# Step sizes moved into the exponents of a state-space scan, and one product per head in place of two

## What is computed

```python
xbc = jax.nn.silu(centred_dwconv(c_xbc, lp['ssm_conv_w']) + lp['ssm_conv_b'])
c_x, c_b, c_c = split_cols(xbc, (D_INNER, SSM_GROUPS * SSM_STATE, SSM_GROUPS * SSM_STATE))
dt = jax.nn.softplus(c_dt.reshape(b, t, 2, SSM_HEADS) + lp['ssm_dt_bias'])
da = dt * (-jnp.exp(lp['ssm_a_log']))
y_f, ss_f = ssd_scan(c_x * dt[:, :, 0, :, None], da[:, :, 0], c_b, c_c, s_ssm0[:, 0])
y_b, ss_b = ssd_scan(rev(c_x * dt[:, :, 1, :, None]), rev(da[:, :, 1]), rev(c_b), rev(c_c), s_ssm0[:, 1])
y = y_f + rev(y_b) + lp['ssm_d'][:, None] * c_x
```

```python
lmat = jnp.exp(jnp.where(lower, acum[..., :, None] - acum[..., None, :], -jnp.inf))
cb = jnp.einsum('bclgn,bcsgn->bcgls', cc, bc)
y_diag = jnp.einsum('bcgls,bcgrls,bcsgrp->bclgrp', cb, lmat, xc)
```

## Time and profile before

| what | value |
| --- | --- |
| median of 3 runs | 3850.91 us |
| range of the runs | 3846.19 to 3855.83 us |
| the profiled execution | 3846.83 us |
| its span, first to last instruction | 3845.1 us |
| mean granted TensorE clock | 0.978 of full speed |
| TensorE busy | 3655.9 us (95%), 29057 matmuls |
| TensorE weight loads | 3441.8 us (90%) |
| VectorE, ScalarE, GpSimd busy | 2042.3, 1087.7, 638.9 us |
| DMA | 506.51 MB, mean 132 GB/s |

### The profile page before, as it was taken

How to read it: one execution, slowest core, us unless ns; L and a number is a source line. 1 busy time by engine, 2 the same in 40 slices (tenths; PEclk the granted TensorE clock), 3 DMA queues, 4 the chain that set the end, 5 groups by cost and what they waited for, 6 DMA issues and landing times.

```text
span 3845.1 us, 68478 instructions
## 1 busy us (share of the span) xinstructions
PE 3655.9 (95%) x29057; PEld 3441.8 (90%) x29057; DVE 2042.3 (53%) x2526; ACT 1087.7 (28%) x1953; POOL 638.9 (17%) x698
## 2 busy tenths in 40 slices
PE   7999999999899899899989999999998998899998
PEld 6999999999888776899989999999997886588998
DVE  5531453233478786585375225523325877856743
ACT  4211111122344562331122102112224456343311
POOL 1111111222400233100011101112233003510000
PEclk8999999999899999999999999999998999999999
DMA  6332233233621387752333332333346114776432
GB/s 242 110 106 92 87 93 95 85 122 109 248 59 39 131 287 247 242 170 76 104 122 102 93 104 76 93 92 108 105 135 210 51 41 166 260 252 189 138 94 91
DMA packets 361201, 506.51 MB, mean 132 GB/s; under 512 B 82528, under 2 KB 284872, under 8 KB 357968
## 3 DMA queue, kind: packets, MB, share of 16 engines
q1 hardware_dynamic: 309880, 375.22, 29.9%
q0 software_dynamic: 35040, 103.09, 8.8%
q10 hardware_dynamic: 16000, 24.12, 1.9%
HBM read 330.62 MB, written 171.73 MB: 131 GB/s over the span
## 4 chain that ended last, share of the span: by engine, by line
PE 70%; DVE 10%; issue 9%; DMA 3%; DVEq 2%; SPq 2%; ACT 2%; POOL 2%; ACTq 0%; POOLq 0%
PE PSUM L833 10%; PE PSUM L835 10%; PE PSUM L834 10%; PE PSUM L1379 4%; PE PSUM L1381 4%; PE PSUM L1380 4%; PE PSUM L1658 4%; PE PSUM L1493 3%; PE PSUM L1480 2%; PE PSUM L1790 2%; PE PSUM L1792 2%; PE PSUM L1791 2%; PE PSUM L1459 1%; SPq L695 1%; PE PSUM L1460 1%
## 5 line engine op out<-in xcount | busy, mean ns | idle before, releaser
L833 PE MATMUL PSUM<-h_hi,w_hi 128*128 128x384 f32 x2304 | 772.1, 335 | 4.4 <-ACT conv_in L1974 1.8
L835 PE MATMUL PSUM<-h_hi,w_lo 128*128 128x384 f32 x2304 | 770.4, 334 | 0.0
L834 PE MATMUL PSUM<-h_lo,w_hi 128*128 128x384 f32 x2304 | 770.4, 334 | 0.0
L833 PEld LDWEIGHTS PSUM<-h_hi,w_hi 128*128 128x128 f32 x2304 | 432.7, 188 | 9.2 <-issue 9.1
L834 PEld LDWEIGHTS PSUM<-h_lo,w_hi 128*128 128x128 f32 x2304 | 432.7, 188 | 0.0
L835 PEld LDWEIGHTS PSUM<-h_hi,w_lo 128*128 128x128 f32 x2304 | 432.7, 188 | 0.0
L2356 POOL DMA_DIRECT2D proj_d<-leave x140 | 131.8, 942 | 1381.3 <-DVE leave L2704 543.1
L1379 PE MATMUL PSUM<-h_hi,w_hi 128*128 128x384 f32 x960 | 325.4, 339 | 0.0
L1380 PE MATMUL PSUM<-h_lo,w_hi 128*128 128x384 f32 x960 | 321.5, 335 | 0.0
L1381 PE MATMUL PSUM<-h_hi,w_lo 128*128 128x384 f32 x960 | 321.5, 335 | 0.0
L2810 DVE TENSOR_REDUCE row_max<-PSUM 128x1 f32<-128x1152 f32 x128 | 173.4, 1355 | 97.6 <-PE PSUM L1460 97.4
(11 more groups left out here) (406 smaller groups left out, 7329.5 us busy)
## 6 DMA issues: line engine op xcount, KB each, us to landing
proj_d<-leave POOLq DMA_DIRECT2D x140, 512.0 KB, 3.9
w_raw<-in_w_in SPq DMA_DIRECT2D x54, 1024.0 KB, 5.5
gdn_tile_d<-g_out SPq DMA_DIRECT2D x18, 1536.0 KB, 6.9
wide_br<-proj_d SPq DMA_DIRECT2D x48, 576.0 KB, 4.4
xs<-ssm_tok_d SPq DMA_DIRECT2D x32, 640.0 KB, 5.7
ssm_tok_d<-x_rest SPq DMA_DIRECT2D x36, 512.0 KB, 3.5
w_in<-in_w_in SPq DMA_DIRECT2D x16, 1024.0 KB, 6.3
av_t<-gdn_tile_d SPq DMA_DIRECT2D x28, 512.0 KB, 5.3
```

The costliest lines, as they stand in the source:

```text
L833: pe.matmul(dst, wh, x_hi[:, k, lo:hi], start=(k == 0), stop=False)
L834: pe.matmul(dst, wh, x_lo[:, k, lo:hi], start=False, stop=False)
L835: last = pe.matmul(dst, wl, x_hi[:, k, lo:hi], start=False, stop=(k == kt - 1))
```

## The change

The step size enters as a logarithm: exp(decay[l] - decay[s] + log dt[s]). Log dt is formed in the projection's decay pieces (Ln, and one correction step with Exp), split in two parts like the decay sums, transposed, and stored as `steprow_d`; a third DMA per direction brings it to rows 64 to 95 of `s_col`, where `s_row` (through `head_of`) has the matching sign. With dt in the exponential, x needs no scaling: VectorE adds the exponentials of both directions and multiplies the sum by `cb`, and y takes one product per head with `xt` as it is. `x_dt` goes, `w_ssm` is one tile, and the exponents go by half of the heads (both directions of a half), where they went by direction. D times x comes after all four exponentials, and x_rest on VectorE after the second half.

The decay pieces of the projection: ScalarE's D_SUMS and D_LAST, TensorE's D_LAST, VectorE's D_TERMS and D_SUMS.

```diff
+                    if run == D_SUMS:
+                        act.wait_ge(decay_term, l * 3 + 2)
+                        act.activation(dec["u"][:, :, 16:48], dec["neg"][:, :, 16:48], ACT.Ln)
+                        act.drain()
+                        act.activation(dec["poly"][:, :, 16:48], dec["u"][:, :, 16:48], ACT.Exp, scale=-1.0).then_inc(decay_exp, 1)
...
+                        act.activation(step_rows[:, 0:3], bank(6, 3 * P, P).rearrange("p (c n) -> p c n", n=P), ACT.Copy)
+                        act.activation(step_rows[:, 3], bank(7, P), ACT.Copy)
+                        act.activation(step_rows[0:64, 4], bank(7, P, P)[0:64], ACT.Copy).then_inc(row_made, 1)
...
+                        for c in range(3):
+                            pe.transpose(bank(6, P, (c + 1) * P), step_cols[:, c * P:c * P + P], ident)
+                        pe.transpose(bank(7, P), step_cols[:, 3 * P:4 * P], ident)
+                        pe.transpose(bank(7, P, P)[0:64], step_cols[:, 4 * P:4 * P + 64], ident).then_inc(decay_prod, 1)
...
+                        dve.tensor_scalar(D["neg"][:, :, 16:48], D["soft"][:, :, 16:48], 1e-37, None, ALU.max)
...
+                        dve.wait_ge(decay_exp, l * 3 + 2)
+                        steps = D["poly"][:, :, 16:48]
+                        dve.tensor_tensor(steps, D["neg"][:, :, 16:48], steps, ALU.mult)
+                        dve.drain()
+                        dve.scalar_tensor_tensor(steps, steps, -1.0, D["u"][:, :, 16:48], ALU.add, ALU.add)
+                        dve.drain()
+                        for d in range(2):
+                            dve.tensor_copy(step_hl[:, :, d, 0], steps[:, :, 16 * d:16 * d + 16])
+                        dve.drain()
+                        for d in range(2):
+                            dve.tensor_tensor(step_hl[:, :, d, 1], steps[:, :, 16 * d:16 * d + 16], step_hl[:, :, d, 0].bitcast(F32), ALU.subtract)
```

SyncE stores the new rows; every engine that waits for the rows waits for seven stores in place of five:

```diff
+                sp.dma_start(flat_steps[0:512].rearrange("(c p) n -> p c n", p=P), step_rows[:, 0:4].bitcast(F32)).then_inc(row_out, 16)
+                sp.dma_start(flat_steps[512:576], step_rows[0:64, 4].bitcast(F32)).then_inc(row_out, 16)
-                sp.wait_ge(row_out, l * 80 + 80)
+                sp.wait_ge(row_out, l * 112 + 112)
```

TensorE in SSM preparation:

```diff
                     for h in range(8 * half, 8 * half + 8):
-                        for d in range(2):
-                            for part in HALVES:
-                                dst = PSUM[part, h * SP_:(h + 1) * SP_]
-                                last = pe.matmul(dst, w_ssm[d][:, h, part], x_dt[p][d][:, h], start=d == 0, stop=d == 1)
+                        for part in HALVES:
+                            last = pe.matmul(PSUM[part, h * SP_:(h + 1) * SP_], w_ssm[:, h, part], xt[p][:, h * SP_:(h + 1) * SP_], start=True, stop=True)
...
-                def exponents(t, d):
+                def exponents(t, half):
                     n = l * NT + t
-                    if d == 0:
+                    if half == 0:
                         for e in range(2):
-                            pe.wait_ge(s_in[e], (n + 1) * 32)
-                    for half in range(2):
-                        if t or d:
-                            pe.wait_ge(sp_e, n * 4 + 2 * d + half - 1)
+                            pe.wait_ge(s_in[e], (n + 1) * 48)
+                    for d in range(2):
+                        if t or half:
+                            pe.wait_ge(sp_e, n * 4 + 2 * half + d - 1)
```

ScalarE, per tile:

```diff
-                    act.wait_ge(sp_cb, n * 2 + 1)
...
-                        for h in ((0, 1, 2, 3, 4, 5), range(6, SH))[d]:
+                        for h in ((), range(SH))[half]:
```

GpSimd, the loads of the next tile's rows and their wait:

```diff
+                    pool.dma_start(s_col[d][64:96], steprow_d[t, d]).then_inc(s_in[d], 16)
...
-                        pool.wait_ge(sp_d, (l * NT + t) * 4 - 2 + 2 * d)
+                        pool.wait_ge(sp_d, (l * NT + t) * 4 - 1 + d)
```

VectorE, per tile:

```diff
-                    times_dt(t, 0).then_inc(sp_cb, 1)
...
-                    times_dt(t, 1)
...
                         for d in range(2):
-                            dve.wait_ge(sp_e, n * 4 + 2 * d + half + 1)
-                            dve.tensor_tensor(w_ssm[d][:, hs], e_ssm[d][:, hs], again(cb[p][:, half], 8), ALU.mult).then_inc(sp_w, 1)
-                        if half == (0 if t else 1):
+                            dve.wait_ge(sp_e, n * 4 + 2 * half + d + 1)
+                        dve.tensor_tensor(e_ssm[0][:, hs], e_ssm[0][:, hs], e_ssm[1][:, hs], ALU.add)
+                        dve.drain()
+                        dve.tensor_tensor(w_ssm[:, hs], e_ssm[0][:, hs], again(cb[p][:, half], 8), ALU.mult).then_inc(sp_w, 1)
+                        if half == 1:
```

77 lines of the change are left out of this document (42 added, 35 removed).

## The result

The changed kernel takes **3859.66 us** (median of 8 runs, 3854.82 to 3871.48). The kernel before, run beside it, takes 3846.49 us (8 runs): the ratio is **1.0035**, 95% interval [1.0025, 1.0044], slower. Measured twice more, the same kernel gave 1.0019 [1.0010, 1.0029] and 1.0008 [0.9998, 1.0018]. The mean of the three is 1.0021, some 8 us; the third interval includes 1. The forecast was 4 us faster, with a range that ended at 3859: the first median lies 0.7 us outside it, those of the two repetitions, 3856.57 and 3857.27, lie inside (beside a kernel before at 3849.74 and 3851.45).

The account below looks back on a forecast made before the run. No engine had much room; the new ring was the wait for step-row loads. Layer 0 +0.8, layer 1 -6.8 (ends included) and projection +1.9 summed to -4.1 us: 3842.7 profiled, 3846.8 as median, range 3835 to 3859.

Parts of the forecast that it names:

- The slower rival: Layer 0, TensorE's s_in wait before each tile's first exponent matmul: third load queues in the burst; 3861.1 us, chance 0.17.
- L: Landing time of a small load in scan preparation; taken as 4.1 us in layer 0 and 2.8 in layer 1.
- five beats of 11.3: Layer 0's scan preparation: five one-tile beats of 11.3 us where each took 11.45, giving -0.8 us.
- 7.2 + L: Scan preparation: beat length, the last load issued 7.2 us after a tile's first exponent matmul starts, plus its landing time.
- Tile 3 in layer 0: Scan preparation: only the stretch from first to last exponent matmul of this tile gets shorter, -1.2 us.
- T8: Scan preparation: end of tile 8's last exponent matmul, where the preparation terms stop and the end term starts.
- The floor of ScalarE's ring: Scan preparation: shortest beat ScalarE's work allows if loads land fast, 10.65 us in layer 0, 9.4 in layer 1.
- E to T: Scan preparation: from start of a tile's first exponent matmul to end of its last, put at 4.8 us.
- Layer 1: Scan preparation of layer 1: tile 3 gives -2.1 us, five beats of 10.0 for 11.45 give -7.5.
- The end: After tile 8's last exponent matmul: stores wait for later x_rest, delaying the scan's second-step loads; +2.8 us per layer.
- The projection: Each layer's projection: one more VectorE operation, +0.37 us, and five more TensorE transposes, +0.6; two layers +1.9.
- D_SUMS on ScalarE at nothing: Projection: extra Ln, Exp and two table loads cost nothing, covered by 12.57 us of idle ScalarE; uncovered 3.7 us.

Follow-up runs that it names:

- two_loads: The changed kernel with the third load (step rows) made for tile 0 alone, later tiles keeping tile 0's step rows; ratio 1.0002 to the kernel before.
- changed_third: The changed kernel measured a third time, unaltered; ratio 1.0008 to the kernel before.
- changed_again: The changed kernel measured a second time, unaltered; ratio 1.0019 to the kernel before.
- before_proj: The kernel before with only the projection part of the change, log dt stored but not read; ratio 1.0009, and 1.0013 when run again.
- late_rest_last: The changed kernel with VectorE's x_rest moved ahead of both halves in tile 8 alone; ratio 1.0028 to the kernel before.
- rest_last_two: The changed kernel with VectorE's x_rest ahead of both halves in tiles 7 and 8, last in the others; ratio 0.9993 to the kernel before.
- xrest_early: The changed kernel with VectorE's x_rest put back behind the first half for every tile but the first; ratio 0.9997 to the kernel before.
- xrest_first: The changed kernel with VectorE's x_rest ahead of the sum of y and both halves in tiles 1 to 8; ratio 1.0001 to the kernel before.
- two_rows: The changed kernel with two buffers of s_row and s_col per direction, rows loaded two tiles ahead; ratio 0.9993 to the kernel before.

## Why the prediction was wrong, point by point

- **The slower rival had the place, and the place only.** TensorE does wait for s_in ahead of the first exponent matmul in layer 0. Its price was built as five equal beats of 12.9 from L = 5.7. Found: a mean of 12.2 to 12.5, made of beats of 11.1 and of 12.5 to 15.4. The third load, which it blamed, is the smaller part (two_loads). That its 3861.1 lies near the first median, 3859.7, is luck.
- **The step that failed: layer 0's "five beats of 11.3", one L for every beat and a wait priced at its length, with the clock at nothing.** The form 7.2 + L was right where the rows are waited for: from tile 4's first exponent matmul to the last issue are 7.4 us (1365.68 to 1373.09), and L was 5.1. That gives 12.6 between first exponent matmuls. The beat measured 15.24, because TensorE's clock came down behind the waits: 7.72 us from first to last exponent matmul where 5.06 is the time at full clock, 2.7 us more. Here 1.25 us of waiting for the rows, close behind the 1.69 ahead of C times B, cost 4.15 us over the short beat. L = 4.1 was not too small in the mean: the five were 3.2, 5.1, 1.8, 4.8 and 1.9. In two beats the rows set the pace, in three ScalarE did (11.1). The five beats together are 5.8 us over 5 x 11.3; the lower clock in tiles 5 and 7 makes 4.2 of it (in changed_third 4.2 of 5.9, in changed_again 2.5 of 4.3), the uneven L the rest.
- **Tile 3 in layer 0** was to give -1.2. In two of three profiles its beat is 12.8 to 12.9 as before, since it too runs at the lower clock (6.6 us from first to last exponent matmul); in the third it is 11.15 at full clock. Layer 0 up to T8: forecast -2.0, found +4.7.
- **The floor of ScalarE's ring** was put at 10.65 and is 11.1 (E to T is 5.05, not 4.8). Since five beats of before take 11.45, this ring alone left only 1.8 us to win in layer 0.
- **Layer 1** came out: -9.6 forecast up to T8, -9.3 found, beats 9.98 to 10.11 for 10.0. TensorE waits there 0.5 to 1.8 us for the rows in tiles 4 to 8 and keeps its clock at 1.00. The wait before it is shorter (0.9 us, for the sum of y); whether that is the reason was not tested.
- **The end**: +2.8 per layer forecast, +3.0 and +3.2 found (+2.6 and +2.5 with before_proj's profiles counted to before). x_rest ends 5.5 us after T8, as said. But the reason was short: tile 8's x_rest isn't enough, tile 7's starts the chain (late_rest_last, rest_last_two). The ends can be shorter than before's 70.2 to 71.0: 68.2 and 72.2 with x_rest in its old place (xrest_early), 68.1 and 68.4 with it first (xrest_first).
- **The projection**: +1.9 forecast, +1.7 found in the stretch where it could be located; by the ratios of its two runs +3.5 and +5 us. TensorE's wait grew from 0.8 to 1.06. D_SUMS on ScalarE at nothing: right. The Trainium skill (ScalarE: Activation LUTs, What ACT_TABLE_LOAD costs) would have had four switches at about 2.66 us each; the trace shows four loads of 1.28 us, beside idle time.
- **What is left open.** The located terms make +3.3 us, the three ratios +3 to +13.5, in the mean +8. The rest lies outside the preparation and the scan, in stretches that are longer in all 16 profiles with the projection part (3498.6 to 3509.3 us) than in the two without (3496.4 and 3493.0), but that also differ by up to 11 us among themselves. What in them reacts to the projection part is open. That the loss would be near zero or gone without either of two things, the load wait or the late x_rest, is shown (two_rows, rest_last_two, both 0.9993).

The sum as forecast, as found:

| term | forecast | found |
| --- | --- | --- |
| layer 0, start to T8 | -2.0 | +4.7 |
| layer 1, start to T8 | -9.6 | -9.3 |
| two ends | +5.6 | +6.2 |
| projection | +1.9 | +1.7 |
| sum | -4.1 | +3.3 |

## What to carry to other kernels

A new wait on an engine whose clock can fall behind it may cost more than its length. Price the work behind it at both clocks, and take more than one profile: in changed_again two waits of much the same length cost 1.4 us over the short beat in tile 4 and 4.0 in tile 6. Small loads that are issued behind the last use of their buffer land in whatever the big transfers leave, so give them a second buffer before the work around them is made shorter. When a source of stores is moved to the end of a step, follow its queue over two steps: what is issued behind the wait for the previous step's stores starts one step earlier than it looks.
